# Prompt attention: on Pool the subtraction that finishes the split of a weight block moves from behind the rounding to behind the next unit's weighings

## What is computed

```python
for start in range(0, tq, SB_BLOCK):            # 128 queries at a time
    z = jnp.einsum('bqhd,bkhd->bhqk', qb, kb) * scale
    mask = kpos[None, :] < qpos[:, None]
    log_one_minus = jnp.where(mask, jax.nn.log_sigmoid(-z), 0.0)
    after = lax.cumsum(log_one_minus, axis=3, reverse=True) - log_one_minus
    a = jnp.where(mask, jnp.exp(jax.nn.log_sigmoid(z) + after), 0.0)
    outs.append(jnp.einsum('bhqk,bkhd->bqhd', a.astype(v.dtype), vb))
```

## The kernel before

| blocks split | unit (w%4, g) of the rounding | weighings just ahead, elements | weighings of the next unit |
|---|---|---|---|
| 2 | the first unit, k = 0 | 639 | 767 |
| 3 to 7 | (1, 0) | 383, 511 | 895 |
| 8 to 10 | (2, 0) | 895 | 1023 |
| 11 to 14 | (2, 1) | 1023 | 127, 255 |
| 15 to 17 | (3, 0) | 127, 255 | 639 |

## Time and profile before

### The profile page before, as it was taken

The page is one execution under the profiler, slowest core; times in us unless marked ns, Lnnn a source line. Parts: engine busy times, 40 slices in busy tenths (PEclk is TensorE's granted clock), DMA queues, the critical chain, the costliest instruction groups (busy, mean ns, idle before and its releaser), DMA issues. The chain is left out here.

```text
span 2292.2 us, 33621 instructions
## 1 busy us (share of the span) xinstructions
PE 2165.7 (94%) x12884; PEld 2055.4 (90%) x12884; DVE 1297.7 (57%) x1733; ACT 754.4 (33%) x1448; POOL 905.7 (40%) x494
## 2 busy tenths in 40 slices
PE   6999999998999899989996989799999999999996
PEld 6999999998899899988995978699999999999995
DVE  5044120003787777856653547667767676676756
ACT  3222102223666667744431122221211212121124
POOL 2335334444644556546662310323242333324223
PEclk9999999999999999999997999899999999999998
DMA  5125324637545454555556442211111111111004
GB/s 173 46 72 188 120 77 117 182 117 184 134 124 137 117 136 122 136 177 145 155 143 193 120 153 92 83 47 46 37 49 34 55 37 46 46 37 54 28 19 167
DMA packets 290827, 237.49 MB, mean 104 GB/s; under 512 B 51142, under 2 KB 267926, under 8 KB 290710
## 3 DMA queue, kind: packets, MB, share of 16 engines
q1 hardware_dynamic: 281968, 222.24, 33.8%
q10 hardware_dynamic: 7510, 9.19, 1.3%
q0 software_dynamic: 1232, 4.46, 0.5%
HBM read 168.51 MB, written 67.33 MB: 103 GB/s over the span
## 5 line engine op out<-in xcount | busy, mean ns | idle before, releaser
L168 PE MATMUL p_psU<-mergedT_lo,p_w_hi 128*128 128x364 f32 x1056 | 346.8, 328 | 3.3 <-ACTq L2233 3.3
L170 PE MATMUL p_psU<-mergedT_hi,p_w_lo 128*128 128x364 f32 x1056 | 347.6, 329 | 0.0
L169 PE MATMUL p_psU<-mergedT_hi,p_w_hi 128*128 128x364 f32 x1056 | 347.3, 329 | 0.0
L148 POOL TENSOR_SCALAR p_w_hi<-p_w_raw 128x1024 fp32r<-128x1024 f32 x72 | 98.1, 1362 | 557.7 <-PE p_psD L170 418.5
L282 PE MATMUL p_psB<-hT_lo,w_hi 128*128 128x364 f32 x888 | 295.6, 333 | 2.4 <-issue 2.4
L282 PE MATMUL p_psB<-hT_hi,w_lo 128*128 128x364 f32 x888 | 293.1, 330 | 0.0
L282 PE MATMUL p_psB<-hT_hi,w_hi 128*128 128x364 f32 x888 | 292.5, 329 | 0.0
L2255 DVE TENSOR_TENSOR p_acc<-p_psD,p_acc 128x512 f32<-128x512 f32 x378 | 260.1, 690 | 42.6 <-PE p_psD L170 41.2
L1136 DVE TENSOR_TENSOR_SCAN p_rest<-p_rest 128x896 f32<-128x896 f32 (+7 forms) x128 | 226.0, 1777 | 91.9 <-ACT p_rest L1069 91.6
L927 POOL TENSOR_TENSOR p_weights<-p_weights,p_rest 128x895 f32<-128x895 f32 (+7 forms) x128 | 170.4, 1340 | 190.8 <-DVE p_rest L1136 190.8
L168 PEld LDWEIGHTS p_psU<-mergedT_lo,p_w_hi 128*128 128x128 f32 x1056 | 199.2, 189 | 5.5 <-POOLq L132 3.4
(11 more groups left out here) (282 smaller groups left out, 4701.9 us busy)
## 6 DMA issues: line engine op xcount, KB each, us to landing
p_w_raw<-in_w_up SPq DMA_DIRECT2D x44, 512.0 KB, 3.6
w_raw<-in_w_in SPq DMA_DIRECT2D x40, 512.0 KB, 3.9
p_w_raw<-in_w_down SPq DMA_DIRECT2D x22, 512.0 KB, 3.5
p_kT<-k_hi_scratch SPq DMA_DIRECT2D x32, 256.0 KB, 4.8
p_kT<-k_lo_scratch SPq DMA_DIRECT2D x32, 256.0 KB, 5.3
w_raw<-in_w_gate SPq DMA_DIRECT2D x16, 512.0 KB, 4.2
p_raw_v<-in_cache_sb_v SPq DMA_DIRECT2D x8, 1024.0 KB, 6.1
p_raw_k<-in_cache_sb_k SPq DMA_DIRECT2D x7, 1024.0 KB, 6.4
```

The lines of the kernel that those rows point to most:

```text
L148: self.nc.gpsimd.tensor_scalar(self.hi[:, slot, :], self.raw[:, parity, :], 1.0, 0.0, ALU.mult, ALU.add).then_inc(self.split, 1)
L168: nc.tensor.matmul(out, stat_hi, mov_lo, start=first, stop=False)
L169: nc.tensor.matmul(out, stat_hi, mov_hi, start=False, stop=False)
L170: return nc.tensor.matmul(out, stat_lo, mov_hi, start=False, stop=last)
```

## The change

In prompt attention the rounding of block n+2 stays where the whole split was, behind the weighings of the unit in which PE finishes block n. The subtraction is issued one unit later, behind the weighings of that unit. `split_one`, which the other stages use, is the same two steps in a row. The wait for the group, the wait for the raw block and the wait for the rounding keep their values; the buffers and the loads are the same.

```diff
--- before.py
+++ after.py
@@ -143,10 +143,18 @@
 
     def split_one(self, pool, n, uses, slot, parity):
 
+        self.round_one(pool, n, uses, slot, parity)
+        self.rest_of_one(pool, n, slot, parity)
+
+    def round_one(self, pool, n, uses, slot, parity):
+
         pool.wait_ge(self.raw_ready[parity], (uses + 1) * 16)
         hold(pool, self.passed)
         self.nc.gpsimd.tensor_scalar(self.hi[:, slot, :], self.raw[:, parity, :], 1.0, 0.0,
                                      ALU.mult, ALU.add).then_inc(self.split, 1)
+
+    def rest_of_one(self, pool, n, slot, parity):
+
         pool.wait_ge(self.split, n * 2 + (self.CREDIT + 1))
         self.nc.gpsimd.tensor_tensor(self.lo[:, slot, :], self.raw[:, parity, :],
                                      self.hi[:, slot, :].bitcast(F32), ALU.subtract).then_inc(self.split, 1)
@@ -959,9 +967,16 @@
                         q_lo(e)
                     for b in scored(k):
                         weigh(b)
+                    for n in range(blocks_ended(k - 1) if k > 1 else 0, blocks_ended(k) if k else 0):
+                        if n + 2 <= DB:
+                            ring.rest_of_one(pool, n + 2, slot(n + 2), (n + 2) % 2)
                     for n in range(blocks_ended(k) if k else 0, blocks_ended(k + 1)):
                         if n + 2 <= DB:
-                            split(n + 2)
+                            pool.wait_ge(s("group"), NCH * (n + 1))
+                            ring.round_one(pool, n + 2, (n + 2) // 2, slot(n + 2), (n + 2) % 2)
+                for n in range(blocks_ended(len(UNITS) - 1), blocks_ended(len(UNITS))):
+                    if n + 2 <= DB:
+                        ring.rest_of_one(pool, n + 2, slot(n + 2), (n + 2) % 2)
 
             @block.tensor
             def _(pe):
```

## The result

Measured: 2315.3 us median (6 runs, 2312.6 to 2318.07) against 2295.78 for the kernel before in the same runs; ratio 1.0083, 95% interval 1.007 to 1.0095. The change makes the kernel 19.5 us slower. The forecast was 2314.5. The profiled execution's span is 2315.6 us against 2292.2, +23.4.

What follows compares the result with a forecast made beforehand. PE paces prompt attention, losing 26.5 us in 20 short waits. Terms 18.0 - 8.8 + 4.9 + 2.7 + 4.1 = +20.9 on 2293.94 gave 2314.8, stated as 2314.5 us; own range 2307 to 2321, 2296 to 2322 for all but the faster case.

Steps and rivals of the forecast that it cites:

- Blocks 3 to 7, +18.0: Five attention heads: later subtraction delays SP's load, stores of y and DVE's additions; 3.6 us per head, +18.0 us.
- Blocks 8 to 10, -8.8: Three attention heads: subtraction goes behind the weighing of 1023 that PE waits for; -3.4, -3.4 and -2.0, sum -8.8 us.
- Blocks 11 to 14, +4.9: Four attention heads: subtraction behind weighings of 127 and 255 delays SP's load and the store DVE awaits; +4.9 us.
- Blocks 15 to 17, 0: Late attention heads: subtraction about 3.5 us later behind a weighing of 639, hidden by PE's lead; 0 us.
- Block 2, +2.7: PE waits for this subtraction, which goes behind the subtraction of q and the weighing of 767; +2.7 us.
- Half clock, +4.1: PE at half clock behind new waits in the heads of blocks 3 to 7: three times 1.4, +4.1 us.
- the subtraction gets the port first: Rival, blocks 3 to 7: subtraction runs before DVE's scan of 1024, SP less late; +6.3 us, 2300; chance 0.15.
- the stores land in time: Rival, blocks 3 to 7: late stores of y land faster, heads lose only 0.8 each; +2.8, 2296.7 us; chance 0.12.
- The faster case: Rival: blocks 8 to 10 give 8.8 us and DVE makes up for SP's lateness; 2284.5 us; chance 0.13.

Runs made afterwards that it cites:

- With SP's load last: The changed kernel with the next block's load issued behind its unit's stores of y and loads of k, q and v: 2288.9 us, ratio 0.9963.
- blocks 11 to 14 alone: The kernel before with only the subtractions of blocks 11 to 14 moved, behind the weighings of 127 and 255: 2304.14 us, ratio 1.0031.
- the kernel before with SP's load last: The kernel before with the next block's load issued behind its unit's stores of y and loads of k, q and v: 2292.01 us, ratio 0.9984.
- blocks 3 to 7 alone: The kernel before with only the subtractions of blocks 3 to 7 moved one unit on: 2318.2 us, ratio 1.0094.
- block 2 alone: The kernel before with only the subtraction of block 2 moved: 2300.25 us, ratio 1.0015.
- blocks 3 to 7 with SP's load last: The kernel before with only blocks 3 to 7's subtractions moved and the next block's load issued last in its unit: 2294.84 us, ratio 0.9993.

## Why the prediction was right, step by step

The forecast was 2314.5 and the median 2315.3. The mechanism is the one forecast, but part of the closeness is luck: the sum was +20.9, the attention accounts for +18.4 in the trace, and the stages behind it, which the forecast left out, differ in the traces by another 5.0 that may be chance.

- *Blocks 3 to 7, +18.0.* The order of events is the one predicted: weighing of 895, scan of 1024 ahead of the subtraction, SP's load behind it, the late store, the late addition. From the rounding to SP's load it is 681.45 - 671.48 = 9.97 us; it was 658.82 - 655.26 = 3.56; so 6.4 later, where 6.7 was predicted. The head lost 3.6, as predicted. The other four were not alike: blocks 4 and 5 lost 5.2 and 4.7, block 7 lost 3.0. With 5.9 - 2.4 for block 3 the five are 20.0; alone they measured 21.5. Of the 5.2 and 4.7, 1.4 each is half clock (below); without it the five are 3.5, 3.8, 3.3, 3.6 and 3.0, 17.2 in all against the 18.0. Inside the head the split was another: the turn came 1.3 us later (a wait of 1.90 for 0.64), not 0.8; the scan of 1024 took 2.38 us where 2.1 was put in.
- *Blocks 8 to 10, -8.8.* -9.8 in the trace (3.6, 3.7 and 2.4 in the three heads, where 3.4, 3.4 and 2.0 were predicted), -9.7 alone. The turn waits 0.24 instead of the 0.5 predicted. The store behind SP's load did not reach PE.
- *Blocks 11 to 14, +4.9.* +5.7 in the trace, +7.5 alone (5.1 to 9.4). Of the 5.7, 1.4 is a half-clock stretch that was not forecast for these heads; the waits themselves cost 1.0 to 1.2 each, as forecast.
- *Blocks 15 to 17, 0.* 0.0 in the trace.
- *Block 2, +2.7.* The split is done 2.4 us later; alone it measured +3.6.
- *Half clock, +4.1.* It was kept as a term of its own: three stretches behind turns of blocks 3 to 7. The trace has six new ones in this stage, besides a second one behind the later split of block 2. Three lie behind turns, in the heads of blocks 3, 5 and 6; the sums that follow wait for a store anyway, and that wait takes them up: the head of block 6 has its stretch there (last section) and still lost 3.6. The other three lie behind sums that waited for the addition, at 599.1, 632.0 and 830.2 us (the heads of blocks 3, 4 and 11), and come through:

```profile
599.60:602.80 3.20, 3.20 (x15) 3.20 (x14) 2.68 (x4) 0.66 (x2) 1.05 (x1) 0.50 0.77 171
...
633.60:636.80 3.20, 3.20 (x13) 3.20 (x12) 1.89 (x4) 1.21 (x4) 1.54 (x1) 0.50 0.79 164
...
831.80:835.00 3.20, 3.20 (x12) 3.20 (x12) 1.72 (x4) 1.15 (x4) 1.54 (x1) 0.52 0.78 164
```

From these sums to the next ones it is 6.45, 6.45 and 6.61 us, against 5.07 behind the sums at 663.62, where the clock stayed at 2.4 GHz: 1.4 to 1.5 each. So about 4.3 us were right as a total, and that is luck: none of them is where the forecast had them.
- *The sum.* Two of its products are rounded loosely (four times 1.2 is 4.8, three times 1.4 is 4.2). Against its 20.9 the terms in the trace are 20.0, -9.8, 5.7, 0.0 and 2.4, together 18.3.
- *The rivals.* That the subtraction gets the port first did not happen: it is listed with 4.38 us. That the stores land in time is refuted by DVE's waits for `yb_scratch`, 47.9 us in 17 where they were 18.1 in 6. The faster case had its first half right (blocks 8 to 10); its second, that DVE makes up for what SP is late, did not happen. With SP's load last the kernel does come near its 2284.5 (2288.9), because the stores go earlier. The rule of the Trainium skill (SBUF — State Buffer, Who interferes with whom), first come, whole instruction, agrees with the rows of this head: the scan was issued 0.18 us ahead of the subtraction and went first.

## What to carry to other kernels

An instruction that moves on one engine moves everything that waits for it, and the longest lever may be a DMA queue: here the load of a block that is rounded two heads later (block 8, loaded at 681.45 and rounded at 736.94) stood ahead of a store for which DVE was waiting 8 us later, from 689.46 on. Put transfers with much slack behind those with little. And when the same work costs nothing in one place of a cycle, as the split of blocks 15 to 17 did, move the others to that place whole before taking them apart.

## What was not expected of the hardware

Waits of PE of 1.8 to 1.9 us were followed by half clock in three of the five heads of blocks 3 to 7, not in all. Behind the wait of 1.90 at 683.55 the granted clock is 0.51 (1.2 GHz); in the stretch at 700.8, with no wait ahead, 1.00 (2.4 GHz):

```profile
684.90:688.20 3.30, 3.30 (x13) 3.11 (x12) 1.84 (x4) 1.53 (x4) 0.00 (x0) 0.51 1.05 261
...
700.80:704.00 3.20, 3.20 (x23) 3.11 (x23) 1.89 (x4) 2.75 (x7) 1.99 (x2) 1.00 0.11 37
```

In the kernel before, waits of 1.1 us were never followed by it, and one of 2.94 was not either. The turn of block 8 waits 2.84 us in six of the traces: half clock follows in those of the kernel before, of blocks 11 to 14 alone and of the kernel before with SP's load last, and not in those of blocks 3 to 7 alone, of block 2 alone and of blocks 3 to 7 with SP's load last. So the length of a wait alone does not tell whether it comes; what it costs was 1.4 us where no later wait took it up.
